# Two transformer blocks in one launch: feed-forward transitions rebuilt, norm sums placed between matmuls, some clock fillers added and some taken away

## The reference

```python
def first_block(x, ...):                      # 2 layers, 256 tokens
    for i in range(2):
        h = rms_norm(x, attn_norm[i])
        x = x + (dsa_mixer if i == 0 else mla_mixer)(h, ...)     # sparse attention, latent attention
        h = rms_norm(x, mlp_norm[i])
        a = relu(h @ w_up); x = x + (a * a) @ w_down             # 1024 -> 4096 -> 1024
    return rms_norm(x, final_norm)

def second_block(x, meta_tokens, ...):        # 16 meta tokens in front: 272 tokens
    h = concatenate([meta, x])
    for i in range(2):
        f = swiglu(rmsnorm(h, ffn_norm_pre[i, 0]), w1, w3, w2)   # 1024 -> 2816 -> 1024
        h = h + 0.5 * rmsnorm(f, ffn_norm_post[i, 0])
        m = pool(rmsnorm(h, ...)) if i == 0 else diff_attention(rmsnorm(h, ...))
        h = h + rmsnorm(m, mix_norm_post[i])
        f = swiglu(rmsnorm(h, ffn_norm_pre[i, 1]), ...)          # the second feed-forward of the layer
        h = h + 0.5 * rmsnorm(f, ffn_norm_post[i, 1])
    return h[:, 16:]
```

## Time and profile before

| | |
|---|---|
| median of 3 runs | 1736.18 us (1717.48, 1736.18, 1741.19) |
| the profiled execution | 1721.73 us, of which span 1719.9 us |
| mean granted TensorE clock of it | 0.994 |
| PE busy | 1656.5 us, 96% of the span |
| DVE busy | 1051.0 us, 61% |
| ACT busy | 757.0 us, 44% |
| DMA | 252.99 MB, mean 147 GB/s |

### The profile page before, as it was taken

One profiled execution on the slowest core, in us unless ns is written; L12 is line 12 of the kernel. 1 busy time (PEld: TensorE's weight loads), 2 busy tenths in 40 slices (PEclk: granted clock), 3 DMA queues, 4 the chain that ended last, 5 costly groups with the idle time before them and its releaser, 6 DMA issues.

```text
span 1719.9 us, 30972 instructions
## 1 busy us (share of the span) xinstructions
PE 1656.5 (96%) x12658; PEld 1548.7 (90%) x12658; DVE 1051.0 (61%) x1261; ACT 757.0 (44%) x1007; POOL 6.4 (0%) x21
## 2 busy tenths in 40 slices
PE   7899999998999999999999999999999999999998
PEld 5858999987899998999987999979999796789997
DVE  7785765458666556666457665466554647576653
ACT  3345553432655434444445444444443336454442
POOL 0000000010000000000000000000000000000000
PEclk9989999999999999999999999999999999999999
DMA  7602566633146675556722556635575351235671
GB/s 168 165 25 74 171 187 180 190 101 105 44 147 194 172 196 167 173 179 185 194 76 90 179 171 190 174 101 171 172 207 158 111 182 51 67 123 180 197 205 61
DMA packets 346674, 252.99 MB, mean 147 GB/s; under 512 B 32574, under 2 KB 345820, under 8 KB 346604
## 3 DMA queue, kind: packets, MB, share of 16 engines
q1 hardware_dynamic: 345136, 250.00, 49.4%
q10 hardware_dynamic: 1468, 2.02, 0.4%
HBM read 250.95 MB, written 1.05 MB: 147 GB/s over the span
## 4 chain that ended last, share of the span: by engine, by line
PE 82%; DVE 12%; ACT 4%; DMA 1%; issue 1%; ACTq 0%; DVEq 0%; SPq 0%
PE acc L457 25%; PE acc L458 25%; PE acc L459 25%; DVE w_low L1313 2%; PE acc L610 2%; PE spare L588 1%; DVE xg_low L1357 1%; ACT w_high L915 1%; PE acc L596 1%; DVE x_state L1508 1%; DVE squares L1342 1%; PE acc L473 1%; DVE evac_a L1506 1%; ACT xg_high L920 1%; PE acc L844 0%
## 5 line engine op out<-in xcount | busy, mean ns | idle before, releaser
L1313 DVE TENSOR_TENSOR w_low<-w_raw,w_high 128x2048 fp32r<-128x2048 f32 (+3 forms) x229 | 540.6, 2361 | 415.5 <-ACT w_high L915 415.4
L457 PE MATMUL acc<-xg_high,w_high 128*128 128x272 f32 (+4 forms) x2592 | 743.9, 287 | 14.7 <-DVE w_low L1313 7.6
L915 ACT ACTIVATE w_high<-w_raw 128x2048 fp32r<-128x2048 f32 (+3 forms) x229 | 451.4, 1971 | 684.4 <-PE acc L459 645.4
L458 PE MATMUL acc<-xg_low,w_high 128*128 128x272 f32 (+4 forms) x2592 | 737.8, 285 | 0.0
L459 PE MATMUL acc<-xg_high,w_low 128*128 128x272 f32 (+4 forms) x2592 | 735.7, 284 | 0.0
L457 PEld LDWEIGHTS acc<-xg_high,w_high 128*128 128x128 f32 (+3 forms) x2592 | 485.9, 187 | 32.0 <-issue 14.4
L458 PEld LDWEIGHTS acc<-xg_low,w_high 128*128 128x128 f32 (+3 forms) x2592 | 484.7, 187 | 3.7 <-issue 3.3
L459 PEld LDWEIGHTS acc<-xg_high,w_low 128*128 128x128 f32 (+3 forms) x2592 | 484.8, 187 | 0.2
L457 PE MATMUL acc<-hidden_high,w_high 128*128 128x256 f32 (+1 forms) x1216 | 345.2, 284 | 2.2 <-DVE w_low L1313 2.1
L459 PE MATMUL acc<-hidden_high,w_low 128*128 128x256 f32 (+1 forms) x1216 | 344.5, 283 | 0.0
L458 PE MATMUL acc<-hidden_low,w_high 128*128 128x256 f32 (+1 forms) x1216 | 344.4, 283 | 0.0
(11 more groups left out here) (198 smaller groups left out, 1062.9 us busy)
## 6 DMA issues: line engine op xcount, KB each, us to landing
w_raw<-in_ffn_w_dram SPq DMA_DIRECT2D x88, 1024.0 KB, 5.3
w_raw<-in_ffn_w_dram SPq DMA_DIRECT2D x32, 1408.0 KB, 7.0
w_raw<-in_mlp_w_up_dram SPq DMA_DIRECT2D x32, 1024.0 KB, 5.4
w_raw<-in_mlp_w_down_dram SPq DMA_DIRECT2D x32, 1024.0 KB, 5.6
w_raw<-in_attn_w_qkv_dram SPq DMA_DIRECT2D x12, 1024.0 KB, 5.1
w_raw<-in_a_w_in_dram SPq DMA_DIRECT2D x18, 256.0 KB, 4.4
w_raw<-in_a_w_in_dram SPq DMA_DIRECT2D x4, 1024.0 KB, 8.1
w_raw<-in_a_w_out_dram SPq DMA_DIRECT2D x4, 1024.0 KB, 5.0
```

The lines of the kernel that those rows point to most:

```text
L457: pe.matmul(dst, high_w, high, start=first, stop=False)
L458: pe.matmul(dst, high_w, low, start=False, stop=False)
L915: act.activation(whi[c % 2][:, 0:SIZES[c]], raw[c % 2][:, 0:SIZES[c]], ACT.Copy).then_inc(S["w_high"], 1)
L1313: dve.tensor_tensor(wlo[c % 2][:, s], raw[c % 2][:, s], whi[c % 2][:, s].bitcast(F32), ALU.subtract)\
```

## The change

**Post norm.** `post_unit` makes the squares first, with a semaphore of its own (post_sq), and the copy to `mixer_out` after them. The squares of the last unit go to a tile `square_last` which DVE doesn't add any more: PE adds it to the sum itself, with another matmul of the ones (`sum_with_last`). This is done at the ends of ffn0 to ffn3, of the pool and of w_o; one to three fillers ahead of the sum go.

**Groups.** The first pair of feature tiles is split into two singles (`FINE`), in `post_norm`, `xg` and PE's waits. Between mlp1 and ffn0, DVE now makes each group's xg_low between the final norm's products, not after all of them.

**Second chunk.** For three matrices (ffn_up2, qkv, ffn_up3) the second chunk gets a third buffer, `w_high_ahead` and `w_low_ahead`, at a free place of the hidden tiles. Its split moves from the first up unit to the last down unit of the matrix before, on ACT and DVE. For ffn_up0 and ffn_up1 only ACT's half moves, ahead of `xg`; DVE's stays behind the folding of squares.

**Norm sum.** In `up`, in a_in and in qkv, `sum_squares` no longer stands between the first and the second unit but behind the first three matmuls of the second (`between`). This holds for mlp0 and mlp1 as well.

**Third chunk.** ACT splits it right behind `root` and loads Silu's table after that, not before.

**Fillers.** 7 before a feed-forward's first unit become 5 (also before the pool and qkv), 3 before the pool's norm sum become 2. In the sparse attention stage some are added: 7 of full width before the turn of v, then 2 of half width ahead of the third scores and 2, 2, 1, 1 of half width ahead of the first four turns of the probabilities.

```diff
+FINE = SINGLES[0:2] + PAIRS[1:]
...
+        ahead = [G[name].c0 + 1 for name in ("ffn_up2", "qkv", "ffn_up3")]
+        def slot(c):
+            return 2 if c in ahead else c % 2
...
+            def sum_with_last(T, groups, tiles):
+                pe.wait_ge(S["sq_read"], n.add("sq_read", groups))
+                pe.matmul(normps[:, 0:T], ones[:], sqsum[:, 0:T], start=True, stop=False)
+                pe.wait_ge(S["post_sq"], n.get("post_sq"))
+                for t in range(tiles):
+                    ins = pe.matmul(normps[:, 0:T], ones[:], sqlast[:, t, 0:T], start=False, stop=t == tiles - 1)
+                ins.then_inc(S["norm_sum"], 1)
...
                         ins = three(acc[u % 2][0:rows_, m, 0:T], *w, XH[:, k, T0:T0 + T], XL[:, k, T0:T0 + T],
                                     k == 0, k == KD - 1)
+                        if between is not None and k == 0 and m == 0:
+                            between()
...
                 wide(g, 0, T0, T, xg_waits(groups))
-                sum_squares(T, 1)
-                wide(g, 1, T0, T)
+                wide(g, 1, T0, T, between=lambda: sum_squares(T, 1))
...
             def ffn(i, T0, T):
-                up(G[f"ffn_up{i}"], T0, T, PAIRS, KF2 // 2, 7)
+                up(G[f"ffn_up{i}"], T0, T, FINE, KF2 // 2, 5)
                 down(G[f"ffn_down{i}"], T, KF2, 1)
-                keep_busy(sp[0][:, 0], 1)
-                sum_squares(T, KD)
+                n.add("post_sq", KD)
+                sum_with_last(T, KD - 1, 1)
...
+                    if p == 1:
+                        keep_busy(acc[0][:, 1], early, 256)
...
+            keep_busy(acc[1][:, 0], 7)
             pe.wait_ge(S["q_ready"], n.add("q_ready"))
...
-                      "exp_done")
+                      "exp_done", [2, 2, 1, 1], 2)
...
                     if first:
                         root(T)
+                    split(g.c0 + j + 2, it, 2)
+                    if first:
                         act.preload_act_table_set("silu_and_others")
-                    split(g.c0 + j + 2, it, 2)
...
-                    if j < KD - 1:
+                    if j < KD - 1 or slot(g.c0 + j + 2) == 2:
                         split(g.c0 + j + 2, it, 2)
...
-                for q in range(4):
-                    t = ta[q % 2][:, :, 0:T]
+                groups = PAIRS if gcol is None else FINE
+                for q, (a, b) in enumerate(groups):
+                    t = ta[q % 2][:, 0:b - a, 0:T]
...
-            squares_after(G["ffn_up2"].c0 + 1, T2)
+            squares_after(None, T2)
```

More of the change, by code:

```diff
@@ L473, in keep_busy, with wide @@
                     pe.matmul(bank[:, 0:width], ones[:], cst[:, 0:width], start=True, stop=True)
-            def wide(g, j, T0, T, ready=None, it=None, per=0, tiles=None):
+            def wide(g, j, T0, T, ready=None, it=None, per=0, tiles=None, between=None):
                 c, u = g.c0 + j, g.u0 + j
@@ L576, in turn_v, with attention @@
                 pe.wait_ge(S["v_ready"], n.add("v_ready", q))
-            def attention(pieces, scores, prob_tiles, values, probs_by, idle=()):
+            def attention(pieces, scores, prob_tiles, values, probs_by, idle=(), early=0):
                 s0, t0, o0 = n.get("s_read"), n.get("pt_ready"), n.get("o_read")
@@ L662, in _ @@
             wide(g, 0, META, SEQ, xg_waits(PAIRS))
-            sum_squares(SEQ, 1)
-            wide(g, 1, META, SEQ)
+            wide(g, 1, META, SEQ, between=lambda: sum_squares(SEQ, 1))
             turn_rope(g, 0, P, 2, rotA)
@@ L1076, in ffn @@
                     unit(j)
-                n.add("squares", KD)
+                n.add("squares", KD - 1)
                 root(T)
@@ L1210, in _ @@
             PRE = GAIN["ffn_norm_pre_2"]
+            split(G["ffn_up0"].c0 + 1)
             xg(PRE, 0, T2)
[L1212 removed]
             ffn(0, 0, T2)
@@ L1239, in _ @@
                 act.wait_ge(S["act_evac"], g.r0 + j + 1)
-                par = n.add("squares") % 2
-                act.wait_ge(S["sq_read"], n.get("squares") - 2)
-                act.activation(sq[par][:], ta[j % 2][:], ACT.Square, scale=D ** -0.5).then_inc(S["sq_made"], 1)
+                if j == 3:
+                    act.activation(sqlast[:], ta[j % 2][:], ACT.Square, scale=D ** -0.5).then_inc(S["post_sq"], 1)
+                else:
+                    par = n.add("squares") % 2
+                    act.wait_ge(S["sq_read"], n.get("squares") - 2)
+                    act.activation(sq[par][:], ta[j % 2][:], ACT.Square, scale=D ** -0.5).then_inc(S["sq_made"], 1)
             root(T2)
+            split(G["ffn_up1"].c0 + 1)
             xg(PRE + KD, 0, T2)
-            split(G["ffn_up1"].c0 + 1)
             ffn(1, 0, T2)
             xg(PRE + 2 * KD, 0, T2)
-            split(G["ffn_up2"].c0 + 1)
             ffn(2, 0, T2)
@@ L1251, in _ @@
             g = G["qkv"]
-            split(g.c0 + 1)
             root(T2)
@@ L1277, in _ @@
             for j in range(4):
-                if j < 3:
-                    split(g.c0 + j + 2)
+                split(g.c0 + j + 2)
                 gc = GAIN["mix_norm_post_2"] + KD + 2 * j
                 post_unit(g, j, [F[:, 2 * j + m, META:] for m in range(2)], acc[(g.u0 + j) % 2],
-                          [gain[:, gc + m:gc + m + 1] for m in range(2)], SEQ, sq0)
-            n.add("squares", 4)
+                          [gain[:, gc + m:gc + m + 1] for m in range(2)], SEQ, sq0, last=j == 3)
+            n.add("squares", 3)
             root(SEQ)
             xg(PRE + 3 * KD, META, SEQ)
-            split(G["ffn_up3"].c0 + 1)
             ffn(3, META, SEQ)
@@ L1370, in squares_after @@
                 fold_squares(4, KD, T)
-                split(then)
+                if then is not None:
+                    split(then)
             def variance(T):
@@ L1884, in _ @@
             for j in range(4):
+                split(g.c0 + j + 2)
                 if j < 3:
-                    split(g.c0 + j + 2)
-                dve.wait_ge(S["act_evac"], g.r0 + j + 1)
-                add_squares(2, SEQ, None)
+                    dve.wait_ge(S["post_sq"], n.add("post_sq"))
+                    add_squares(2, SEQ, None)
+            n.add("post_sq")
             variance(SEQ)
```

102 lines of the change are left out of this document (57 added, 45 removed).

## The result

The changed kernel took 1720.64 us (median of 20 runs, 1716.93 to 1724.11), the kernel before in the same job 1734.64 (20 runs, 1716.23 to 1741.19). The ratio of their runs is 0.9948, 95% interval 0.9924 to 0.9971. The forecast was 1715.6, range 1705 to 1733. The time lies inside the range. The way to it does not fit: the forecast's sum was a gain of 6.1 us, the medians differ by 14.0, and neither half of this result is where the forecast had it.

What follows compares the result with a forecast made beforehand. PE, busy in 96% of the span, was taken as the bound, with gains only where it waits or runs fillers. Gains of 9.7 less losses of 3.6 gave 6.1 us: 1721.73 to 1715.6 us, range 1705 to 1733.

Steps and rivals of the forecast that it cites:

- the forecast's sum: Whole kernel: gains of 9.7 us less losses of 3.6, net 6.1 us, taken from the profiled 1721.73 us.
- the clock's: Transitions: two clock falls before, costing 3.1 us, and two falls expected again, so zero.
- the fillers, put at 1.3: Sparse attention stage: half-width fillers cost 1.5 us (bounds 0 and 3.5); the seven full ones +0.4, clock -0.6.
- sparse attention at half clock: Slower rival: PE, saturated there, runs at half clock; from 20.6 us of it the whole exceeds 1736; chance 0.05.
- the higher level stays: Rival: a cause outside the edited places keeps most new runs at the higher level, 1730 us (1725 to 1735); chance 0.22.
- Second chunk, sum and third chunk in ffn2, qkv and ffn3: Earlier split removes a wait, third unit starts sooner: gains 2.7 (4.2 with the clock's fall), 2.65 and 3.05 us.
- mlp0 and mlp1: The sum moves behind PE's wait for w_low, so the third unit starts later: loss 0.7 us in each.
- The prices of 0.8 and 0.1: Losses in ffn0 (0.8 us) and ffn1 (0.1 us) as the sum stands behind PE's wait for w_low.
- Worth nothing by itself: Groups: PE's first matmul comes some 2.4 us earlier without gain, since DVE sets the first unit's end.
- Falls of the clock in all five rebuilt transitions: Rival: three more falls than the forecast has, 4.6 us, giving 1720 us; chance 0.13.
- It doesn't do what it says: Rival: the chunk split ahead lands late or holds up ACT; without the 8.4 us gain, 1724; chance 0.07.

Runs made afterwards that it cites:

- e1: The kernel before, unchanged, run again: 1735.33 us, ratio 1.0020; its profiled run took 1737.04 us.
- e3: The changed kernel without the added sparse-stage fillers: 1735.30 us, ratio 1.0021 to the kernel before.
- e6: The changed kernel without the seven full-width sparse-stage fillers, keeping the eight of half width: 1722.29 us.
- e2: The kernel before with only the new sparse-stage fillers added: 1719.88 us, ratio 0.9955.
- e11: e8 with the second chunk of ffn_up2, qkv and ffn_up3 split in the first up unit again, norm sum before the second unit: 1721.84 us.
- e4: The changed kernel with the norm sum ahead of the second unit again in mlp0, mlp1, ffn0 and ffn1: 1718.08 us, ratio 0.9951.
- e13: The changed kernel with only the tile square_last moved behind the hidden tiles: 1716.18 us.
- e8: e4 with pairs of feature tiles in place of singles, and seven fillers again ahead of each first unit: 1715.51 us, ratio 0.9898.
- e10: e8 with square_last placed behind the hidden tiles, same instructions: 1709.34 us, ratio 0.9898 to the kernel before.
- e9: e2 with an unused tile of square_last's size at that tile's place, same instructions: 1725.78 us.
- e15: e10 with an unused tile of 2048 bytes directly ahead of the hidden tiles: 1713.11 us.

## Why the prediction was right or wrong

- **The steps that failed, in short.** (1) Nothing in the sum stood for the upper group: the forecast took the lower level as its start, without a row that shows why the new kernel would stay there. All of the 14.0 us between the medians is this. (2) The sum of 6.1 us came out as nothing beside the lower group, by three terms: the clock's, put at nothing, where the falls behind the moved sums alone cost 4 us; the fillers, put at 1.3, where this profile has 3.3; and the place of the new tile, which was not in the sum at all (4.5 us by the medians, 0.5 in this pair of profiles). The time of 1720.6 inside the range is therefore in part luck.
- **The level.** The forecast started from the profiled execution (1721.73), which is of before's lower group, and so gave a time near 1720 while the shown median was 1736. That was right for the time. Wrong was the step that left the cause open and put the sparse attention at half clock among the rivals as a mishap of the *new* kernel ("it ran at 1.00 with no fillers"). It was the state of the *old* kernel in 90 of 153 runs, and the fillers ended it (e1 to e3). The rival's size was near (20.6 us was its mark, 17 was measured); its sign was reversed. The rival "the higher level stays" named the condition, the clock in the sparse stage, correctly.
- **Second chunk, sum and third chunk in ffn2, qkv and ffn3.** Right in the mechanism, and in size for two of the three. ffn2 gained 4.1 for 4.2, both with the 1.5 of before's fall in it. qkv gave 2.0, with a fall of the clock in its new first unit; e3 and e6, without one there, give 2.5 for 2.65 against e2. ffn3 gave 3.05, the number that was forecast, but 1.6 of it is a fall that before had and the forecast did not count here: e6 and e3 give 2.1 and 2.4 against e2. The third unit of ffn2 starts 6.3 us after the sum, where 6.2 was worked out. e11 shows the split ahead by itself.
- **mlp0 and mlp1.** Right: 0.8 and 0.9 us lost for 0.7 each, though the wait at the third unit is 0.23 where 0.5 was expected.
- **ffn0, ffn1 and the clock.** The prices of 0.8 and 0.1 held but for the clock. The step that failed is the clock's term, put at nothing (two falls before, two again). The wait of 2.5 us was foreseen in both places, but the clock fell behind it in both, and twice more in the first units of qkv and ffn3: four falls, 5.3 us for 3.1, with about 2 us in each of ffn0 and ffn1. e4, which undoes the wait, has ffn0's unit back at 6.1 us. In other executions of the same order ffn1's second unit was spared (e3, e6, e13: 6.7 us, behind a wait of 1.7 to 1.8, after a fall inside the first unit).
- **Fillers.** Priced at 1.3 net; the attention ended 3.3 later in this profile, and the logarithm of mlp0_up started 1.9 later in e2's. Their value, 17 us in three runs of five, was not in the sum.
- **Groups.** "Worth nothing by itself" was right for DVE's time but not for the clock: with waits of 0.5 to 1.2 us in the first unit, the matmuls of qkv's from 1355.4 on start 0.22 to 0.23 us apart, and later 0.125. All profiles together show it: each of the seven with singles has one or two falls in the first units of ffn2, qkv and ffn3, and none of the eight with pairs and the split ahead has one. With pairs and the two fillers (e8) the median is 2.6 us under e4's; that was not tried in one job, and pairs and fillers were not tried apart.
- **The term that was missing.** Nothing in the sum stood for the place of the new tile. It costs 4.5 us in the changed kernel (e13), 6.2 with pairs (e10) and 5.9 in the kernel before (e9), by medians of different jobs. With it out of the way, e13 stands at 1716.18, where 1715.6 was forecast: 6.2 under the lower group of its job (1722.4), but 3.9 under that of all jobs (1720.0), so part of this agreement is chance. In the pair of profiles above the place hardly shows (0.5 us), since before itself had one long MLP stage and the new one a short stage in ffn3.
- **The other rivals.** Falls of the clock in all five rebuilt transitions, 1720: it gives the measured time, and the falls came in four of them (ffn0, ffn1, qkv, ffn3, not ffn2), but they explain only part of it; e13's profile has four too (there in ffn2 and not in qkv), and its median is 1716. "It doesn't do what it says" is refuted by ffn2's rows.

## What to carry to other kernels

Run the kernel before until its own groups show, and profile one run of each: here the median's 14 us were the group, and the edits that were meant for 6 us showed nothing. When a change adds a tile, see which tiles it moves; count the matmuls per us in stages that the edit doesn't touch, since a busy engine at full clock can still be slower (682 for 708 matmuls in 80 us here). Compare stage by stage before crediting an edit with a difference of two profiles. Where a sum or any short step is queued behind a wait of an in-order engine, it lengthens that wait (1.48 to 2.53 us in ffn1) and can take the clock of the unit behind it.

## What was unexpected in the hardware

- A saturated TensorE can stay at its lower clock: 18.00 of 18.00 us busy at 0.50 in e1 and e3, in stretches of 37.5 and 47.8 us at that level. Eight half-width fillers at the head of the stage decided it (e6). They fill 1.2 to 1.6 us of idle time there. That the idle time is the cause is not shown, and why before has it in both groups is open.
- The clock fell behind all seven waits of 2.5 us in front of a second unit, and behind 10 of 37 waits of 1.5.
- Matmuls of 256 columns, whose moving tiles (those with the tokens) lie in SBUF at a step of 1024 bytes, start each 0.113, 0.117 or 0.120 us in the MLP down stages, by where the hidden tiles begin within 256 bytes. At the better places either of the first two occurs by chance and then holds for nearly a whole stage (88.0 and 91.2 in e15). In ffn3's down stage both occur at either kind of place. Why is open. Stages of 272 columns show it hardly: ffn0's down stage took 66.47 us in e10 and 66.51 in e8.
- The change of ACT's table costs 1.28 us and nothing more, before and after: the next instruction starts 0.01 to 0.02 us behind it. The Trainium skill (ScalarE: Activation LUTs, What ACT_TABLE_LOAD costs) has about 2.66 with a drain; the trace disagrees.
